# Between two expert layers: two norms, a pooling mixer and the router's logits as one pipeline over token tiles

## The reference

```
for i in range(DEPTH_2):
    f = mla_mixer(...) if i % 2 == 0 else pool_mixer(x, pool_w, pool_b, pool_scale)
    x = layer_norm(ALPHA * x + f, ln_g[i, 0], ln_b[i, 0])
    f = hier_moe(x, ...)                      # router logits, top 2 experts in a group
    x = layer_norm(ALPHA * x + f, ln_g[i, 1], ln_b[i, 1])

def pool_mixer(x, w, b, scale):
    # four groups of 256 channels, windows 2, 4, 8, 16:
    # mean of the last `win` tokens (fewer at the start), less x
    pooled = concat(means) - x
    return (einsum('bsgc,gcd->bsgd', pooled, w) + b) * scale
```

## Time and profile before

| | us |
|---|---|
| median of 3 runs | 3705.11 (3702.21 to 3709.64) |
| the profiled execution | 3703.39 |
| its span, first to last instruction | 3701.6 |
| PE busy | 2990.1 (81%) |
| DVE busy | 1230.5 (33%) |
| ACT busy | 755.0 (20%) |
| POOL busy | 421.7 (11%) |

### The profile page before, as it was taken

One profiled execution on the slowest core, in us unless ns is written; L12 is line 12 of the kernel. 1 busy time (PEld: TensorE's weight loads), 2 busy tenths in 40 slices (PEclk: granted clock), 3 DMA queues, 4 the chain that ended last, 5 costly groups with the idle time before them and its releaser, 6 DMA issues. The chain is left out here.

```text
span 3701.6 us, 41055 instructions
## 1 busy us (share of the span) xinstructions
PE 2990.1 (81%) x16033; PEld 1764.6 (48%) x16051; DVE 1230.5 (33%) x2023; ACT 755.0 (20%) x1274; POOL 421.7 (11%) x392
## 2 busy tenths in 40 slices
PE   6999879897999999988999895987774157876770
PEld 3455478445888878764555453332221153322220
DVE  1036668213111123322555435110112863111116
ACT  3011222113121212334333311110011220110002
POOL 0000055112000000110000001110100251111002
PEclk9999989898999999999999996998897588998995
DMA  6401000312111133221000015799996236999984
GB/s 262 146 17 34 17 1 1 148 32 88 45 51 45 51 113 97 86 92 54 6 7 4 35 56 217 316 420 419 418 415 267 78 123 267 419 420 420 416 359 194
DMA packets 187464, 615.90 MB, mean 166 GB/s; under 512 B 39248, under 2 KB 101775, under 8 KB 131871
## 3 DMA queue, kind: packets, MB, share of 16 engines
q1 hardware_dynamic: 168862, 580.02, 40.0%
q0 software_dynamic: 18432, 33.60, 2.5%
HBM read 592.56 MB, written 54.53 MB: 175 GB/s over the span
## 5 line engine op out<-in xcount | busy, mean ns | idle before, releaser
L2509 PE MATMUL psum<-moe_ring,hreg 128*32 128x512 f32 x3072 | 387.2, 663 | 145.1 <-DMA moe_ring<-in_moe_w 143.4
L2509 PEld LDWEIGHTS psum<-moe_ring,hreg 128*32 128x32 f32 x3072 | 116.2, 121 | 412.4 <-issue 323.0
L2594 DVE TENSOR_TENSOR ex_hb<-ex_sil,psum 128x256 f32<-128x256 f32 x64 | 27.0, 421 | 642.1 <-ACT ex_sil L2566 642.1
L1068 PE MATMUL psum<-h_hi,gu_hi 128*128 128x512 f32 x704 | 217.6, 390 | 9.2 <-DVE gu_lo L1109 9.2
L1068 PE MATMUL psum<-h_lo,gu_hi 128*128 128x512 f32 x704 | 217.2, 390 | 0.0
L1068 PE MATMUL psum<-h_hi,gu_lo 128*128 128x512 f32 x704 | 217.2, 390 | 0.0
L2541 PE MATMUL psum<-moe_ring,hreg 128*32 128x512 f32 x1728 | 192.1, 597 | 16.2 <-issue 12.1
L485 PE MATMUL psum<-h,pj_w 128*128 128x512 f32 x448 | 194.1, 592 | 0.8 <-ACTq L514 0.8
L2566 ACT ACTIVATE ex_sil<-psum 128x256 f32<-128x256 f32 x64 | 24.6, 384 | 632.1 <-PE psum L2509 632.1
L1068 PEld LDWEIGHTS psum<-h_hi,gu_hi 128*128 128x128 f32 x704 | 132.5, 188 | 36.8 <-issue 9.4
L1068 PEld LDWEIGHTS psum<-h_lo,gu_hi 128*128 128x128 f32 x704 | 132.5, 188 | 27.6
(11 more groups left out here) (467 smaller groups left out, 4825.2 us busy)
## 6 DMA issues: line engine op xcount, KB each, us to landing
moe_ring<-in_moe_w SPq DMA_DIRECT2D x288, 1024.0 KB, 20.9
x<-in_moe_w SPq DMA_DIRECT2D x96, 1024.0 KB, 21.8
draw<-in_w_down SPq DMA_DIRECT2D x44, 512.0 KB, 3.6
XF<-in_w_ada SPq DMA_DIRECT2D x16, 1024.0 KB, 6.4
ln_y<-yrow SPq DMA_DIRECT2D x16, 1024.0 KB, 9.6
x<-xrow SPq DMA_DIRECT2D x24, 512.0 KB, 11.4
gu_raw<-in_w_gate SPq DMA_DIRECT2D x22, 512.0 KB, 3.8
gu_raw<-in_w_up SPq DMA_DIRECT2D x22, 512.0 KB, 3.8
```

The source lines that it names most:

```text
L1068: last = pe.matmul(ps[4 * s + 2 * j + h][:, :], w[j][:, k, :], x[:, k, h * 512:(h + 1) * 512], start=k == 0 and n == 0, stop=k == KD - 1 a ...
L2509: last = pe.matmul(ps[i][r, :], xT[i][:, k, r], ring[n % RING][:, j, kk * 512:(kk + 1) * 512], start=k == 0, stop=k == KD - 1)
L2594: dve.tensor_tensor(hb[i][:, :], sil[q % 2][:, :], ps[i][:, DE:2 * DE], ALU.mult).then_inc(hbd, 1)
```

## The change

Parts 1 to 3 and the choice of experts become one block, `between_experts`, which runs as a pipeline over the eight tiles. The moving mean, less the token itself, is now a product of the normalised tile with a banded 128 x 128 matrix, plus a narrow product (16 columns) with the tile before it. The norm's gain and the mixer's scale are multiplied into the mixer's weights once; its bias row enters PSUM as a product of a row of ones with `c`. The mean is taken from an accumulator of the sum, the variance by a square on ACT with the mean as bias. POOL only fills two constants. `HT` is no longer written; its space holds tile buffers. Loads of `y` have four buffers. The band matrices come as a further constant input, and one more load of eight short rows (the gain by channel) stands at the program's start. `moe` of layer 1 gets an empty `later`.

```
-        layer_norm(nc, K, A, "ln1_", 0, 1, None, combine=True)
-        pool_mixer(nc, K, A)
-        K.clear()
         R = routing_buffers(nc, K, "ro1_", (4, 5), ((0, 4), (4, NT)))
-        layer_norm(nc, K, A, "ln2_", 1, 0, K.xrow, router=1, R=R)
-        moe(nc, K, A, 1, R, R.calls)
+        between_experts(nc, K, A, R)
+        moe(nc, K, A, 1, R, ())
+def between_experts(nc, K, A, R):
...
+            def _(sp):
+                def load(t):
+                    if t >= NX:
+                        sp.wait_ge(summed, t - NX + 1)
+                    sp.dma_start(y[t % NX][:, :, :], src[t]).then_inc(y_in[t % NX], 16)
+                    sp.dma_start(X[:, t, :], K.xrow[t * P:(t + 1) * P, :]).then_inc(x_in[t], 16)
+                def store(t):
+                    sp.wait_ge(out, t + 1)
+                    sp.dma_start(K.xrow[t * P:(t + 1) * P, :], X[:, t, :]).then_inc(stored, 16)
+                load(0)
...
+                for t in range(1, NX):
+                    load(t)
...
+                for t in range(NT + 2):
+                    if NX <= t + 1 < NT:
+                        load(t + 1)
+                    if t >= 2:
+                        store(t - 2)
...
+            def _(dve):
+                def total(t):
+                    dve.scalar_tensor_tensor(out=X[:, t, :], in0=X[:, t, :], scalar=ALPHA, in1=y[t % NX][:, 0, :], op0=ALU.mult, op1=ALU.add)
+                    dve.drain()
+                    dve.scalar_tensor_tensor(out=X[:, t, :], in0=y[t % NX][:, 1, :], scalar=K.GT[:, 1, t:t + 1], in1=X[:, t, :],
+                                             op0=ALU.mult, op1=ALU.add, accum_out=s1[:, t:t + 1])
...
+                for u in range(NT + 2):
+                    if u < NT:
+                        total(u)
+                    if u == 0:
+                        weights()
+                    if u >= 2:
+                        gain_and_bias(u - 2)
+                    if u < NT:
+                        first_scale(u)
+                    if 1 <= u <= NT:
+                        add(u - 1)
+                    if u < NT:
+                        residual(u)
+                    if 1 <= u <= NT:
+                        second_scale(u - 1)
+                dve.wait_ge(R.br_in, 32)
+                for first, last in R.calls:
+                    dve.wait_ge(lg, last)
+                    choose_experts(dve, K, R, first, last)
...
+            def _(act):
+                gate(0)
+                for u in range(NT + 2):
+                    if u + 1 < NT:
+                        gate(u + 1)
+                    if u < NT:
+                        first_root(u)
+                        first_norm(u)
+                    if u >= 2:
+                        copy_turned(u - 2)
+                    if 1 <= u <= NT:
+                        second_root(u - 1)
+                    if u < NT:
+                        copy_pooled(u)
+                    if 1 <= u <= NT:
+                        second_norm(u - 1)
...
+            def _(pe):
+                def pooling(t):
+                    pe.wait_ge(norm1, t + 1)
...
+                    for k in range(KD):
+                        if t == 0:
+                            last = pe.matmul(at, n_[0][:, cols], bands[:, g, P:2 * P], start=True, stop=True)
+                        else:
+                            pe.matmul(at, n_[t % NN][:, cols], bands[:, g, 0:P], start=True, stop=False)
+                            last = pe.matmul(at[:, 0:16], n_[(t - 1) % NN][:, cols], bands[:, g, 2 * P:], start=False, stop=True)
+                def mix(t):
...
+                    for h in range(2):
+                        pe.matmul(ps[2 + h][:, :], one[:, :], c[:, h * 512:(h + 1) * 512], start=True, stop=False)
+                        for g in (2 * h, 2 * h + 1):
+                            for k in range(2):
+                                last = pe.matmul(ps[2 + h][:, (g % 2) * 256:(g % 2 + 1) * 256], PM[t % 2][:, 2 * g + k, :], w[:, g, k, :],
+                                                 start=False, stop=g % 2 == 1 and k == 1)
...
+                for u in range(NT + 2):
+                    if 1 <= u <= NT:
+                        mix(u - 1)
+                    if u >= 2:
+                        turn(u - 2)
+                    if u < NT:
+                        pooling(u)
+                    if u >= 2:
+                        logits(u - 2)
```

More of the change, by code:

```diff
@@ L122, in dft_table, with band_table @@
     return np.stack([np.cos(a), np.sin(a)], 1).astype(np.float32)
+def band_table():
+    i = np.arange(P)
+    t = np.zeros((P, len(WINS), 2 * P + 16), np.float32)
+    for g, win in enumerate(WINS):
+        back = i[None] - i[:, None]
+        inside = (back >= 0) & (back < win)
+        t[:, g, 0:P] = inside / win - np.eye(P)
+        t[:, g, P:2 * P] = inside / np.minimum(i + 1, win)[None] - np.eye(P)
+        t[:, g, 2 * P:] = (back + P < win)[:, 0:16] / win
+    return t
 def modulation(nc, K, A):
@@ L160, in _ @@
                     at += n
+                sp.dma_start(rows[at:at + KD, :], A["ln_g_2"][0, 1].rearrange("(a p) -> a p", p=P)).then_inc(small, 16)
                 for j in range(4):
@@ L174, in _ @@
             def _(pe):
[L175 removed]
+                pe.wait_ge(small, 16 * (len(vecs) + 10))
                 pe.transpose(K.ps[7][:, 0:NCOL], rows[:, :], ident[0:NCOL, 0:NCOL]).then_inc(rows_t, 1)
@@ L2876, in _ @@
+                sp.wait_ge(stored, 16 * NT)
+            @block.gpsimd
+            def _(pool):
+                pool.memset(eps[:, :], LN_EPS)
+                pool.memset(one[:, :], 1.0).then_inc(ones, 1)
             @block.vector
             def _(dve):
[L2878 to L2888, removed]
+                def total(t):
+                    dve.wait_ge(x_in[t], 16)
+                    dve.wait_ge(gated, t + 1)
+                    dve.scalar_tensor_tensor(out=X[:, t, :], in0=X[:, t, :], scalar=ALPHA, in1=y[t % NX][:, 0, :], op0=ALU.mult, op1=ALU.add)
@@ L2893, in _ @@
                     dve.drain()
[L2894 to L2914, removed]
+                    dve.tensor_single_scalar(m1[:, t:t + 1], s1[:, t:t + 1], -1.0 / D, ALU.mult).then_inc(summed, 1)
+                def weights():
+                    dve.wait_ge(mix_in, 16 * 6)
+                    for g in range(4):
+                        for k in range(2):
+                            dve.scalar_tensor_tensor(out=w[:, g, k, :], in0=w[:, g, k, :], scalar=K.cols[:, COL_LN + 2 * g + k:COL_LN + 2 * g + k + 1],
+                                                     in1=sc[:, g * 256:(g + 1) * 256], op0=ALU.mult, op1=ALU.mult)
+                    dve.tensor_single_scalar(ga[:, :], ga[:, :], ALPHA, ALU.mult)
+                    dve.wait_ge(row_in, 32)
+                    dve.tensor_tensor(pb[:, :], pb[:, :], sc[0:1, :], ALU.mult)
+                    dve.drain()
+                    dve.scalar_tensor_tensor(out=c[:, :], in0=c[:, :], scalar=ALPHA, in1=pb[:, :], op0=ALU.mult, op1=ALU.add).then_inc(ready, 1)
@@ new lines, in turn, with logits @@
+                def turn(t):
+                    pe.wait_ge(out, t + 1)
+                    if t >= 1:
+                        pe.wait_ge(copied, 2 * t)
+                    for h in range(2):
+                        for k in range(4):
+                            last = pe.transpose(ps[6 + h][:, k * P:(k + 1) * P], X[:, t, (4 * h + k) * P:(4 * h + k + 1) * P], ident)
+                        last.then_inc(turned, 1)
+                def logits(t):
+                    pe.wait_ge(copied, 2 * t + 2)
+                    if t == 0:
+                        pe.wait_ge(wr_in, 32)
+                    bank, at = R.place[t]
+                    for k in range(KD):
+                        last = pe.matmul(ps[bank][:, at * NR:(at + 1) * NR], xT[t % 2][:, k, :], wr[:, k, :], start=k == 0, stop=k == KD - 1)
+                    last.then_inc(lg, 1)
```

147 lines of the change are left out of this document (120 added, 27 removed).

## The result

| | before | changed |
|---|---|---|
| median time, us | 3706.09 (4 runs, 3702.21 to 3709.64) | 3659.53 (4 runs, 3655.02 to 3663.86) |
| profiled execution: time, span | 3703.4, 3701.6 | 3655.02, 3653.2 |

The ratio is 0.9877, with a 95% interval of 0.9862 to 0.9892: 46.6 us less. The forecast of 3646 had the direction and most of the size. It was 13.5 us too low, and the time lies above its own range (3637 to 3656), within the wide one (3634 to 3668).

The account below looks back on a forecast made before the run. No engine was full between the expert layers; PE would become the bound at 12.3 us a tile. First weight load at 139.1 plus 63.6 put the refill at 202.7 instead of 261.7: 59.0 gained, 3646 us, range 3637 to 3656.

Parts of the forecast that it names:

- Start: From the first load between the expert layers to pooling of tile 0: 21.0 us, with loads at 420 GB/s.
- PE, cold: Pooling and mixer of tiles 0 and 1, PE's clock starting at 1.2 GHz: from 21.0 to 43.8 us.
- PE per tile at 2.4 GHz: Steady pipeline: mixer 3.4, bias products 1.7, pooling 4.1, turn 1.1, logits 2.0; 12.3 us a tile, PE the bound.
- Way round: From a mixer's end over DVE and ACT to pooling two tiles on: 10.9 to 11.9 us, 1.5 spare, not binding.
- The expert start keeps its old distance: Rival: gathers unhurt by ring loads, 53.7 + 1.4 us replace 63.6, and pooling at its lower bound; 3631 us, chance 0.08.
- Tail and choice: After mixer 7 at 117.6: last tile to 125.5, choosing experts 13.2 us to 138.7, block end at 139.1.
- lost collision: In choosing experts, the cast of L2164 would no longer meet POOL's memset: 0.17 us instead of 2.33.
- the last leg: From the expert weights' first load to the weight ring's first refill: forecast 63.6 us.
- What is late next: Weight loads start after choosing; first load to first refill takes layer 0's 63.6 us, not 53.7 from the choice; refill at 202.7.
- PE stays at 1.2 GHz: Rival: PE's clock stays down in the new block, 22 to 24 us a tile; 3715 to 3728 us, chance 0.04.

Follow-up runs that it names:

- the split run: Changed kernel with each one-partition bias product split into two of 256 columns, placed behind its group's full-height products: 3670.33 us, ratio 0.9899 to the kernel before.

## Why the prediction was right, and where it was not

- *Start.* Forecast 21.0, measured 23.2. DMA moved 357 GB/s in the mean and not 420: the mixer's weights were there at 13.7 instead of 11.0, and tile 1's y, for which ACT waits before it turns to tile 0's root, at 17.5 instead of 15.
- *PE, cold.* This term failed, by "the clock was at 1.00 some 5 us after PE began". That came from a mixer without one-partition products. (By it the term would be 7.6, 5 us cold and half of the other 5.2, not the 7.3 that the sum has.) Mixer 0 took 11.1 us in one profile and 9.0 in the other, and mixer 1 fell back to 0.50 and took 9.7 instead of 5.1. At full height mixer 0 takes 7.1, 7.0 and 5.3 in three profiles.
- *PE per tile at 2.4 GHz.* Forecast 12.3, measured 12.14 where the clock is up (mixer with bias 5.9, forecast 5.1; transposes 0.9, pooling 3.5 and logits 1.9, forecast 1.1, 4.1 and 2.0). That the sum comes so near is luck in part: the mixer was 0.8 too short and the others 0.9 too long. What failed is that I held the clock at 1.00 for all tiles: three turns at 13.8. Mixer 7 ended at 132.8, not 117.6; of these 15.2 us some 2 come from the start, 8 from mixers 0 and 1 and 5 from the three dips.
- *Way round.* Not binding, as forecast; 11.65 us where it is bare, inside the forecast's 10.9 to 11.9, and its terms (accumulator read 0.08, no doubling) stayed within the bounds. The Trainium skill's rule weighed in the forecast (Vector Engine (DVE) Microarchitecture Reference, "Points that are easy to get wrong") would have shown in L2953: with the accumulator it takes 1.284 us, against 1.28 without, so the accumulator halves nothing here. (In the rival *The expert start keeps its old distance* the sum takes pooling at 4.1 where the text takes its lower bound, 1.9; with that it is 10.05 a tile, not 11.1.)
- *Tail and choice.* From mixer 7's end to the choosing 7.8 (forecast 7.9), then 13.3 (forecast 13.2), with the cast at 0.17. But the 2.2 us that the forecast books as a lost collision only moved to L2296 in the last leg. The sum held all the same, since its 63.6 us come from layer 0, where that operation (L2280, at 2265.28) takes 2.35 us too. What it costs in the last leg wasn't tried.
- *What is late next.* 62.2 against 63.6, a slip that gave 1.4 us back. That the gathers make it longer than the old 53.7 is not shown: DVE's ranking (L2305, before L2289) alone starts 5.1 us behind the choice's end instead of 3.1. Over all profiles it is 62.2 to 65.3, without a pattern that I can name.
- *The rival "PE stays at 1.2 GHz"* had the right quantity and the wrong cause. Its evidence against, that the clock had stayed up in the old mixer, came from full-height products alone. Only with the bias products doubled does the gain go, at 3704. The longest stretch at 0.50 with work on PE in any profile is 42 us (the split run).

The miss is shown by the height alone: with it made full, the first weight load comes at 136.1 and the refill at 201.4 (forecast 139.1 and 202.7), and the time is 3641. So the height costs some 18 us, and it makes the dips of mixers 4 to 7, where PE never waits. In mixers 0 and 1, where it waits, the share of the one-partition products and that of the waits are not told apart.

The Trainium skill, TensorE: Matmul & The Clock Gate, section "Step-by-step: what each phase is for", says of loading the stationary operand that its time goes by the columns and not by the row count. The trace agrees: loading the ones takes 184 ns with one row and 190 with 128 (medians of 32). So the load's own time isn't what the full height gained. What differs is when the next one starts: behind a one-partition product the load for the next full-height product comes 0.76 us after the last load's end (2907.01), behind a full-height one 0.24 (2931.33). That goes with the shorter half turn; the clock is a matter of its own.

## What to carry to other kernels

A bias row added by a one-partition matmul costs more than its columns: it can lower TensorE's clock for the full products around it (here 18 us in all). Pad it to full height with zeros, or put it where an engine waits anyway, and read the granted clock wherever TensorE never waits, not only where it does. At the start of a pipeline, look for what stands ahead of tile 0 on each in-order engine.

## What the runs showed of the hardware that I had not expected

- TensorE, busy without a gap, went from 2.4 to 1.2 GHz behind a 1-partition product over 512 columns (twice 0.5 us), and with two such in a row from mixer 1 on in every turn.
- Zeros are enough: 127 of 128 rows of the padded bias product are zero, and the clock stays at 1.00 for 81 us.
- 195 transposes of the identity, one behind the other, brought the clock from 0.50 to 1.00 within 5 us and held it for the 18 us that they still lasted.
- A half turn with a one-partition product is 0.35 us longer at the same clock than with a full-height one (2.98 and 2.64).
- A DVE cast of four columns took 2.33 us until four memsets of POOL had ended, and 0.39 when these had drains between them. Another small DVE operation took 2.36 instead of 0.16 in the same way.
